# Attention heads of an encoder: values as the stationary side in windowed heads, probabilities divided before they are turned, output products set between the last heads

## What is computed

```
s = where(valid, q @ k.T * HEAD_DIM**-0.5, -inf)          # window: |q_pos - k_pos| <= 128
m = maximum(s.max(-1), sink);  p = exp(s - m)
p = p / (p.sum(-1) + exp(sink - m));  ya = p @ v          # 8 windowed heads
a = softmax(q1 @ k1.T) - lam * softmax(q2 @ k2.T)         # 4 differential heads
yd = rms_norm(a @ vd, subln_g) * (1 - lambda_init)
x = x + g_m * (concat([ya, yd], -1) @ w_out)
```

## Time and profile before

| | |
|---|---|
| median of 3 runs | 1364.37 us (1362.79 to 1368.64) |
| the profiled execution | 1363.22 us, span 1361.5 us |
| PE, DVE, ACT busy | 1288.9, 452.0, 292.9 us |
| layer 0: first scores to first matmul of out(1,0) | 88.69 to 140.92 us |
| layer 1: first scores to the last turn before out(1,0) | 460.92 to 509.59 us |
| mean granted TensorE clock | 0.984 of full |

### The profile page before, as it was taken

One profiled execution on the slowest core, in us unless ns is written; L12 is line 12 of the kernel. 1 busy time (PEld: TensorE's weight loads), 2 busy tenths in 40 slices (PEclk: granted clock), 3 DMA queues, 4 the chain that ended last, 5 costly groups with the idle time before them and its releaser, 6 DMA issues.

```text
span 1361.5 us, 21859 instructions
## 1 busy us (share of the span) xinstructions
PE 1288.9 (95%) x9514; PEld 714.5 (52%) x9515; DVE 452.0 (33%) x808; ACT 292.9 (22%) x524; POOL 32.8 (2%) x82
## 2 busy tenths in 40 slices
PE   5999999999999989996689999999999999899997
PEld 5766888787888677441233333444354333244342
DVE  4876867777459665200100120001001110000011
ACT  3346544443433462110010000010010000010010
POOL 1102100000001010000000000000000000000000
PEclk9999999999999999998789999999999999899999
DMA  9988748888436757999999999999999999999996
GB/s 349 326 338 329 233 176 311 311 297 309 174 123 208 307 204 306 378 408 424 418 421 423 422 421 419 403 408 421 423 419 421 421 424 421 419 420 421 422 423 259
DMA packets 93044, 481.95 MB, mean 354 GB/s; under 512 B 8808, under 2 KB 10928, under 8 KB 63248
## 3 DMA queue, kind: packets, MB, share of 16 engines
q1 hardware_dynamic: 88992, 475.06, 86.9%
q10 hardware_dynamic: 2720, 2.93, 0.8%
q0 software_dynamic: 1232, 2.50, 0.8%
HBM read 477.32 MB, written 1.05 MB: 351 GB/s over the span
## 4 chain that ended last, share of the span: by engine, by line
PE 82%; DMA 9%; DVE 4%; SPq 2%; ACT 2%; issue 1%; POOL 0%; DVEq 0%; ACTq 0%
PE ps L2621 31%; PE ps L2671 15%; PE ps L2304 8%; PE ps L2306 8%; PE ps L2305 8%; DMA raws<-in_moe_w_down_dram 5%; DMA raw<-in_moe_w_gate_dram 2%; DMA weights<-in_ada_w_dram 2%; SPq L891 2%; PE ps L2687 2%; PE ps L2638 1%; DVE weights_lo L1376 1%; PE ps L2594 1%; PE ps L2385 1%; PE ps L2226 1%; PE ps L2370 1%
## 5 line engine op out<-in xcount | busy, mean ns | idle before, releaser
L2621 PE MATMUL ps<-raw,hX 128*32 128x384 f32 (+3 forms) x3840 | 473.0, 543 | 11.8 <-DMA raw<-in_moe_w_up_dram 8.4
L2621 PEld LDWEIGHTS ps<-raw,hX 128*32 128x32 f32 (+1 forms) x3840 | 162.0, 117 | 296.6 <-issue 267.3
L2671 PE MATMUL ps<-raws,m_actT 128*32 128x512 f32 (+1 forms) x1072 | 168.5, 604 | 9.9 <-DMA raws<-in_moe_w_down_dram 9.9
L2304 PE MATMUL ps<-weights_hi,hT_hi 128*128 128x512 f32 (+1 forms) x416 | 162.1, 390 | 2.6 <-DVE hT_lo L1482 1.4
L1797 DVE TENSOR_TENSOR m_act<-m_act,ps 128x512 f32<-128x512 f32 (+1 forms) x28 | 17.4, 621 | 432.0 <-PE ps L2621 431.2
L2306 PE MATMUL ps<-weights_hi,hT_lo 128*128 128x512 f32 (+1 forms) x416 | 159.0, 382 | 0.0
L2305 PE MATMUL ps<-weights_lo,hT_hi 128*128 128x512 f32 (+1 forms) x416 | 158.6, 381 | 0.0
L1376 DVE TENSOR_TENSOR weights_lo<-weights,weights_hi 128x2048 fp32r<-128x2048 f32 (+1 forms) x52 | 113.1, 2202 | 2.3 <-ACT weights_hi L1052 1.1
L2671 PEld LDWEIGHTS ps<-raws,m_actT 128*32 128x32 f32 (+1 forms) x1072 | 52.2, 123 | 116.3 <-issue 103.5
L1052 ACT ACTIVATE weights_hi<-weights 128x2048 fp32r<-128x2048 f32 (+1 forms) x48 | 87.2, 1840 | 55.9 <-PE ps L2306 51.3
L2304 PEld LDWEIGHTS ps<-weights_hi,hT_hi 128*128 128x128 f32 x416 | 78.2, 188 | 21.0 <-issue 4.8
(11 more groups left out here) (282 smaller groups left out, 1084.3 us busy)
## 6 DMA issues: line engine op xcount, KB each, us to landing
raw<-in_moe_w_gate_dram SPq DMA_DIRECT2D x64, 1024.0 KB, 16.5
raw<-in_moe_w_up_dram SPq DMA_DIRECT2D x64, 1024.0 KB, 22.1
raws<-in_moe_w_down_dram SPq DMA_DIRECT2D x32, 2048.0 KB, 24.7
raw<-in_moe_w_gate_dram SPq DMA_DIRECT2D x64, 768.0 KB, 23.3
raw<-in_moe_w_up_dram SPq DMA_DIRECT2D x64, 768.0 KB, 21.1
raws<-in_moe_w_down_dram SPq DMA_DIRECT2D x28, 1536.0 KB, 19.5
weights<-in_ada_w_dram SPq DMA_DIRECT2D x19, 2048.0 KB, 10.0
weights<-in_ffn_w_gate_dram SPq DMA_DIRECT2D x14, 1024.0 KB, 5.1
```

Source lines behind the costliest of these rows:

```text
L2304: pe.matmul(dst, stat_hi, hi, start=start, stop=False, skip_group_check=True)
L2621: mm = pe.matmul(ps[tile * q:tile * q + tile, bank, 0:COL[n]], hX[:, i, at_row:at_row + tile], raw[buffer][:, at:at + COL[n]], start=(i == ...
L2671: mm = pe.matmul(ps[tile * q:tile * q + tile, bank, col:col + w], stationary[:, at_row:at_row + tile], rows_in[:, D * j + w * g:D * j + w ...
```

## The change

In the windowed heads the product with the values is turned round: `v` (64 columns) is now the stationary side and the turned probabilities of two heads (256 columns) stream, so one pair needs 4 matmuls instead of 16 of 64 columns (8 for each unit), and the output comes out with head columns on the partitions, which is the form that out(c,t) needs. Since 1/sum can no longer be applied to such an output, DVE divides the probabilities first (four `tensor_scalar` on 128x256). ACT writes the output's high half and DVE its low half straight into `hT`. So `turn_rows_of` for units 0 and 2 goes, with its halves. PT has two buffers, by pair. A differential pair turns both units' probabilities in one group of four, copied by one ACT instruction. The mask is added to 128 of the 256 keys only. The squares of the differential outputs move from ACT to DVE. All seven copies of turned queries and keys (`qkT`) are on ACT; DVE made three. The eight k of out(0,0) are put in four pieces among the last attention steps, `keep(5, 2)` goes, and in layer 0 the last two ADA chunks move one step later. The halves of chunk 1's weights are made after the last turn in layer 0; in layer 1 the first half of them is made earlier (`OUT_SECOND_EARLY`). Code for an earlier start of the attention is there but off (`HEAD_EARLY` is False twice).

```diff
+HEAD_EARLY = (False, False)
+ADA_STEP = [[0, 1, 2, 3, 4, 5, 7, 8], [1, 2, 3, 4] if HEAD_EARLY[1] else [0, 1, 2, 3]]
+OUT_SECOND_EARLY = (False, True)
...
             def attention(layer):          # ACT
+                for j in range(2 if early else 0, PAIRS + 3):
+                    k = j - 2
+                    if j == PAIRS:
+                        turned_high(3 * layer + 1, 1)
+                    if 0 <= k < PAIRS:
+                        copy_probs(k, 0)
+                    if k >= 1 and windowed(k - 1):
+                        window_high(k - 1)
+                    if 0 <= k < PAIRS and windowed(k):
+                        copy_probs(k, 1)
+                    if j < PAIRS:
+                        exponentials(layer, j)
+                    if j == PAIRS and OUT_SECOND_EARLY[layer]:
+                        straight_part("out", layer, 1, 0)
+                turned_high(3 * layer + 1, 3)
+                if not OUT_SECOND_EARLY[layer]:
+                    straight_part("out", layer, 1, 0)
+                straight_part("out", layer, 1, 1)
...
-                    then(dve.tensor_tensor(rows, rows, mask[:, t, :].unsqueeze(1).broadcast_to([P, 4, SEQ]), ALU.add))
+                    far = slice(P - t * P, 2 * P - t * P)
+                    then(dve.tensor_tensor(rows[:, :, far], rows[:, :, far],
+                                           mask[:, t, far].unsqueeze(1).broadcast_to([P, 4, P]), ALU.add))
...
-                    dve.reciprocal(rec[:, q, :], den[:, q, :]).then_inc(probs_done, 1)
+                    then(dve.reciprocal(rec[:, q, :], den[:, q, :]))
+                    for n in range(4):
+                        i = dve.tensor_scalar(E[:, par, n, :], E[:, par, n, :], rec[:, q, n:n + 1], None, ALU.mult)
+                    i.then_inc(probs_done, 1)
...
             def head_out(layer, j):
                 if m < 4:
+                    of, hi, lo = window_rows(j)
+                    i = dve.tensor_tensor(lo, of, hi.bitcast(F32), ALU.subtract)
...
                     if j == PAIRS + 2:
+                        turned_low(3 * layer + 1, 3)
+                        if not OUT_SECOND_EARLY[layer]:
+                            low_of("out", layer, 1, 0)
...
                     if windowed(j):
                         for kt in range(NT):
+                            for h in range(2):
+                                mm = pe.matmul(ps[HEAD * h:HEAD * h + HEAD, j % 2, 0:2 * P], v[:, kt, col:col + HEAD],
+                                               turned[:, :, 2 * h + kt, :], start=(kt == 0), stop=(kt == NT - 1),
+                                               skip_group_check=True)
```

More of the change, by code:

```diff
@@ L287, with windowed, turned_at @@
 QK_TILES = 14
+TURN_PAIRS = [(3, 5, 4, 0, 2, 6, 1) if early else tuple(range(QK_TILES // 2)) for early in HEAD_EARLY]
+ROPES_OF_PAIR = (4, 4, 4, 4, 6, 6, 8)
+PAIRS_OF_STEP = ((3, 5), (4, 6), (0, 2), (1, 2))
+BEFORE_HEAD = [IN_ORDER.index((3, 1)) if early else len(IN_ORDER) for early in HEAD_EARLY]
 def pair(i):
     return (i + 4) % 8
+def windowed(j):
+    return pair(2 * j) < 4
+WINDOW_STEPS = [j for j in range(PAIRS) if windowed(j)]
+COPIES_BEFORE = [sum(1 + windowed(i) for i in range(j)) for j in range(PAIRS + 1)]
+def turned_at(n, i):
+    before = 10 * (n // 3) + (0, TURNS, TURNS + NT)[n % 3]
+    return before + (i // 2 if n % 3 == 1 else i) + 1
 Signals = collections.namedtuple(
@@ L1624, in attention @@
             def attention(layer):
-                for m in range(1, QK_TILES // 2, 2):
-                    dve.wait_ge(qkT_ps, 7 * layer + m + 1)
-                    dve.tensor_copy(qkT[:, 2 * m:2 * m + 2, :],
-                                    ps[:, 3, :].rearrange("p (m n) -> p m n", m=2)).then_inc(qkT_odd, 1)
-                for j in range(PAIRS + 3):
+                for j in range(2 if HEAD_EARLY[layer] else 0, PAIRS + 3):
                     if j < PAIRS:
@@ L2361, in scores_of, with turn_probs @@
                     mm.then_inc(s_ps, 1)
-                def turn_probs(i):
-                    u, j = UNITS * layer + i, i // 2
+                def turn_probs(j, half):
+                    turned = COPIES_BEFORE[PAIRS] * layer + COPIES_BEFORE[j] + half
                     pe.wait_ge(probs_done, PAIRS * layer + j + 1)
-                    if i:
-                        pe.wait_ge(pt_done, u)
-                    for n in range(4 if pair(i) < 4 else 2):
+                    if j or half:
+                        pe.wait_ge(pt_done, turned)
+                    for n in range(4):
+                        row = 2 * (n // 2) + half if windowed(j) else n // 2
@@ L2378, in values @@
                     if j >= 2:
                         pe.wait_ge(o_done, PAIRS * layer + j - 1)
-                    for h in range(2 if m < 4 else 1):
-                        width = HEAD if m < 4 else P
-                        col = (m // 2) * HEAD if m < 4 else P + (m - 4) * P
-                        to = (i % 2) * P + h * width
+                    turned = PT[j % 2]
+                    if windowed(j):
+                        col = (m // 2) * HEAD
                         for kt in range(NT):
-                            mm = pe.matmul(ps[:, j % 2, to:to + width], PT[:, i % 2, 2 * h + kt, :],
-                                           v[:, kt, col:col + width], start=(kt == 0), stop=(kt == NT - 1))
```

278 lines of the change are left out of this document (173 added, 105 removed).

## The result

| | before | changed |
|---|---|---|
| median | 1365.39 us (1362.79 to 1368.75, 8 runs) | 1373.17 us (1369.86 to 1375.15, 8 runs) |
| span profiled | 1361.5 us | 1371.3 us |
| mean granted clock | 0.984 | 0.977 |
| layer 0: first turn of queries to layer 1's | 372.23 us | 379.94 us |
| layer 1: first turn of queries to the first matmul on `pick` (start of the expert block) | 82.32 us | 82.55 us |

The ratio is 1.0054, 95% interval 1.0042 to 1.0065: slower by 0.4 to 0.65%, above the forecast of 1362.6 and its range of 1356.5 to 1369. Of the profile's 9.8 us, 0.3 lie ahead of L0, 7.7 in it, 0.2 in L1 and 1.6 behind it; the medians are 7.8 us apart.

A forecast was written before the change was run, and what follows sets the result against it. PE was taken to bound layer 0, the softmax chain partly layer 1's attention, the weight stream the expert block. Layer 0's -0.55, layer 1's -4.0 and the clock's +2.8 gave -1.75: 1362.6 us, range 1356.5 to 1369.

The forecast's parts named there:

- PE's work: Attention of each layer: windowed values, `keep`, turns of `xn` and differential pairs together take 5.7 us less on PE.
- One tile after another (1.86): Windowed values: the two 64-column tiles don't overlap, 1.86 us per pair against 1.07; rival at 1366.7 us, chance 0.12.
- a change of tiling mode adds nothing: Windowed pairs: 16 more mode changes cost nothing beyond the 1.07 us; at 0.1 us each, 1.6 us would go.
- The wait for chunk 1's halves in layer 0: Before out(1,0), layer 0: PE waits 4.75 us for halves queued behind the last turn, leaving a gain of 0.55.
- The waits inside the attention, layer 0: Before turns of probabilities: ADA chunks cover all but two waits, pairs 5 (1.1) and 6 (0.85); +0.1 to +0.4 us.
- The waits inside the attention, layer 1: Before turns of probabilities: one wait grows to 2.9 us at pair 6; sum 6.5 for 6.8, -0.3 us.
- One sign that I had named for being wrong: Layer 1 attention: the forecast is wrong if scores to last turn shrinks by under 4 us.
- nothing of layer 1 reaches the end: Layer 1: expert weights' first two chunks still wait for `down_lo`, so no gain arrives; rival at +2.3 us, chance 0.05.
- The clock: Layer 0, after the wait before out(1,0): 5.7 us of work at 1.2 GHz in place of 2.4, +2.8 us.
- the second kind: Layer 1: the clock also falls after pair 6's 2.9 us wait, +2.8 us; rival at 1365.4 us, chance 0.13.
- L0: forecast +2.25: Layer 0: out(1,0) starts at 140.35 against 140.92, -0.55 us, and a fall of the clock adds 2.8.
- L1: forecast -4.0: Layer 1: out(1,0) waits 1.95 us in its middle and ends at 511.95 against 515.95, counted in full.

The follow-up runs named there:

- e1: Changed kernel with DVE's `mod_round`, which frees the ADA chunks' bank, moved right behind the maxima in both layers; 1366.28 us, ratio 1.0013 to the kernel before.
- e3: Changed kernel with both halves of chunk 1's weights made inside the attention (steps 8 and 9), both layers; 1361.99 us, ratio 0.9974 to the kernel before.
- e6: Changed kernel with early `mod_round`, both chunk 1 halves early, and k = 0 to 3 of out(0,0) ahead of pair 6's turn; 1353.01 us, ratio 0.9906.
- b1: Kernel before, with layer 0's halves of chunk 1 put behind those of the last turned units on ACT and DVE; 1373.76 us, ratio 1.0056.
- e8: Changed kernel with `mod_round` behind the division and ahead of the squares, both layers; 1370.49 us, ratio 1.0035 to the kernel before.
- e7: Changed kernel with 13, 20, 12 and 8 unread identity products filling PE's four long waits; 1367.17 us, ratio 1.0007 to the kernel before.
- b2: Kernel before with the mask added to 128 keys of each tile, not all 256; 1363.86 us, ratio 0.9986.
- e5: Changed kernel with `mod_round` right behind the maxima and both chunk 1 halves made inside the attention; 1357.26 us, ratio 0.9939 to the kernel before.
- e4: Changed kernel with 28, 40, 24 and 16 unread identity products in PE's four long waits, outlasting them; 1377.54 us, ratio 1.0088 to the kernel before.

## Why the prediction was wrong

The forecast was 1.75 us less, and L0 and L1 took 7.9 us more. Two of its steps failed: one wait of PE, 3.67 us before an ADA chunk in layer 0, wasn't in it at all, and the clock's term had one fall where there were four. The rest of its mechanism held, term by term:

**PE's work: right to 0.3 us in a layer.** From the first scores to the end of the last turn, without the waits that the rows show and without the falls of the clock, PE's work went from 50.1 to 44.7 us in layer 0 and from 42.7 to 37.2 in layer 1: -5.4 and -5.5, where I had -5.7. One tile after another (1.86) was false: the windowed product came out at 1.01 us per pair against the 1.07 taken. Two small readings were off. A windowed unit before cost 0.93 on average in layer 0, not the 0.97 of the one row that I read. And I held that a change of tiling mode adds nothing, since the scores' price includes it. It stands in the row ahead. The rule of the Trainium skill, "TensorEngine Tiling (Array Packing)", Key Properties, is that such a change drains TensorE; the trace agrees, at about 0.1 us where a full tile gives way to a narrower one. In the changed kernel a turn of four takes 0.49 from start to start ahead of a full-width float32 product:

```profile
100.15 0.66 PE L2457 MATMUL ps<-ident,E 128*128 128x128 f32 x4
100.64 1.06 PE L2479 MATMUL ps<-v,PT_even 128*128 128x128 f32 x8
```

Ahead of a windowed product it takes 0.58 to 0.59 in all three places of layer 0 (114.79 to 115.38 above is one), and so it does in e1, e3 and e6. That the drain is the cause isn't tested by itself. At 0.1 for each of the four windowed pairs it is 0.4 us a layer, half of the 1.6 us in all that I had named and left out. With the long waits gone, e6 shows the gain at the end: 5.4 us of L0 and 6.9 us of L1, the latter in part from shorter waits.

**The wait for chunk 1's halves in layer 0: right.** Forecast 4.75, measured 4.90; b1 and e3 show cause and price (6.8 us of L0 when it is put in alone, and 6.0 us of L0 when it is taken out, each with its fall of the clock).

**The waits inside the attention, layer 0: this step failed.** I wrote that "in layer 0, PE's ADA chunks cover all but two waits". I used the chunks as cover and never asked what a chunk itself waits for. Pairs 5 and 6 did wait 1.05 and 1.13 (forecast 1.1 and 0.85). But the fifth chunk needs a PSUM bank that DVE lets go at the end of a step, behind all that the change gave DVE. It had no slack before, readable from 107.68 + 0.68 and 108.50, 0.14 us apart. The change took 1.9 from PE's side and put 1.8 on DVE's: 3.67. e1 removes it, e8 removes a part by the amount of the squares.

**The waits inside the attention, layer 1: right.** Pair 6's turn waited 3.07 (forecast 2.9), out(1,0) 2.15 (1.95). Waits before turns of probabilities sum to 3.4 + 3.4 = 6.8 (forecast 6.5), by the waits of PE in layer 1 of the changed kernel:

```profile
PE ps L2457 <- DVE E L1677: 3.4, 3, 1.7
PE ps L2457 <- DVE E L1669: 3.4, 2, 3.1
```

They answer to the earlier trace rows. The first scores come 0.2 us later behind `qkT`, as I allowed, in each layer. One sign that I had named for being wrong did come: from the first scores to the last turn is 3.6 us shorter (48.67 before, 45.11 now), under the 4 us. A fall of the clock of 1.6 us lies inside; without it, it is 5.2. Of the rivals, that nothing of layer 1 reaches the end was false: e3 and e6 are 5.6 and 7.1 us shorter in L1 than the changed kernel, and the stretch behind is no longer for it (825.5 and 824.5 against 825.2).

**The clock: a term mis-sized.** I counted one fall at 2.8 us. That one cost 2.1, because 2.7 us of its half-clock time fell into the wait itself, against 1.4 in the rows that I took the price from (those rows, read as means of the two levels, put the fall at 1178.7 and the rise at 1185.5, not 2.85 us in and at 1185.7, which changes little). And there were four, which cost 6.4 together by e7. I had the second kind as a rival (0.13) and held it off with a row of the kernel before in which PE was at 5.95 of 10 without a fall. b1 and b2 show that this row was no proof: the same stretch, with the same or with smaller waits, fell in their profiles.

**The sum again.** L0: forecast +2.25; with the missed wait 3.67, its fall 1.6, a cheaper second fall -0.7, 0.2 + 0.15 for `qkT` and the longer wait, and 0.3 for PE's work it makes 7.5, measured 7.7. L1: forecast -4.0; two falls of the clock +3.3, 0.3 + 0.2 + 0.2 for the waits and `qkT`, and 0.2 for PE's work make it +0.2, measured +0.2. So the change lost what it gained on PE to three long waits and what followed them. What stays open is 0.2 us in L0.

## What to carry to other kernels

When an engine's work is shortened, go through everything that it waits for, those instructions included that were counted as cover for other waits, and write down the slack of each in the trace before, less what a signal takes; what looked like 0.14 us here was none, and became a wait as soon as either side moved. Where a buffer's release stands at the end of a step, behind new work, put it first: moving three lines was worth 0.4%, and placing the weights' halves in the steps that have room 0.8%. Prefer useful matmuls as filler for a wait (e6) to products that nobody reads (e7), since a long wait here often cost clock as well.

## What was not expected of the hardware

The granted clock fell to 0.50 not only after waits of 4 to 5 us with nothing on PE. It fell in layer 1 after waits of 3.07 and 2.15 (the changed kernel), after one of 1.75 (e3, windows 487 to 492), after 1.58 and 1.24 close together (b1), and in b2 where the longest wait was 1.2. It didn't fall in other profiles with the same waits: 3.08 and 2.2 in e1 (e5 has the same 3.07 and fell), 1.6 and 1.2 in the kernel before, and a wait of 2.01 in layer 0 in e8 passed without one. How much a fall costs varies too: behind the same wait of 3.67 it was 1.6 us in the changed kernel and about 2.4 in e3. So one profile without a fall doesn't show that a stretch is safe from it. What decides between the two isn't settled by these runs.

A product of the identity with itself, 128x128 in float32, cost 0.23 us each in a long row of them (e4). Each leaves two records, so the ten records of `keep` in the earlier trace rows are five products at much the same price; e4's counts would have fitted at half of it.

Four divisions of 128x256 on DVE took 1.05 us from the first's start to the next instruction's, above the 0.9 that one instruction of their total size would suggest, and within the bound of 1.35.
